# A feed-forward that starts its output blocks by chunks, one weight tile per reciprocal, and constant matmuls around a layer norm's broadcast

## The reference

```python
def _conv_ffn(h, w_up, conv_w, conv_b, w_down):
    gate, val = jnp.split(h @ w_up, 2, axis=-1)          # D_FF = 2816
    gate = lax.conv_general_dilated(gate, conv_w[:, None, :], (1,), ...) + conv_b
    return (jax.nn.silu(gate) * val) @ w_down

# a layer, for x and (in layer 0) for the context
x = _layer_norm_2(DEEPNORM_ALPHA * x + g1 * y, ln1_g, ln1_b)
h = x * (1.0 + sc2) + sh2
x = _layer_norm_2(DEEPNORM_ALPHA * x + g2 * _conv_ffn(h, ...), ln2_g, ln2_b)
# layer 0 before its attention: q and k get an RMS norm per head of 64, then a rotation
qa = _rope(_rms_norm_2(_heads(qa, 8, 64), q_gain), cos, sin)
```

## Time and profile before

| | us |
|---|---|
| median of 3 runs | 1800.74 (1795.88 to 1807.39) |
| the profiled execution: its time | 1801.82 |
| its span | 1800.0 |
| PE busy | 1646.7, 91% |
| DVE busy | 940.6, 52% |
| ACT busy | 745.1, 41% |
| granted TensorE clock, mean | 0.962 |

### The profile page before, as it was taken

The page is one execution under the profiler, slowest core; times in us unless marked ns, Lnnn a source line. Parts: engine busy times, 40 slices in busy tenths (PEclk is TensorE's granted clock), DMA queues, the critical chain, the costliest instruction groups (busy, mean ns, idle before and its releaser), DMA issues.

```text
span 1800.0 us, 37019 instructions
## 1 busy us (share of the span) xinstructions
PE 1646.7 (91%) x14957; PEld 1326.6 (74%) x14957; DVE 940.6 (52%) x1712; ACT 745.1 (41%) x1411; POOL 170.8 (9%) x270
## 2 busy tenths in 40 slices
PE   6888899896898988999999899999998999989997
PEld 6675678695666665867666788788875877879997
DVE  5743663486623223264665655335534564578584
ACT  6231444453211124423764533323334556565454
POOL 0020010004000000100431100000001002210000
PEclk9999999997999999999999899999998999989998
DMA  6598777769599998212002222222222240235552
GB/s 248 182 243 280 263 256 250 271 196 265 224 406 407 401 361 296 89 59 83 2 13 82 70 94 94 94 94 94 94 82 71 94 141 13 72 120 181 183 174 71
DMA packets 84418, 302.04 MB, mean 168 GB/s; under 512 B 10080, under 2 KB 12128, under 8 KB 84128
## 3 DMA queue, kind: packets, MB, share of 16 engines
q1 hardware_dynamic: 80144, 288.92, 45.9%
q0 software_dynamic: 2736, 7.35, 1.7%
q10 hardware_dynamic: 1376, 3.47, 0.5%
HBM read 345.56 MB, written 3.15 MB: 194 GB/s over the span
## 4 chain that ended last, share of the span: by engine, by line
PE 77%; DVE 10%; DMA 4%; ACT 4%; issue 3%; POOL 0%; ACTq 0%; SPq 0%; DVEq 0%
PE bank L941 51%; PE bank L900 13%; PE bank L1435 5%; DMA ring<-wall 4%; PE bank L1470 3%; PE bank L1455 3%; PE bank L965 2%; DVE w_lo L2194 2%; ACT w_hi L1684 1%; DVE BIG L2820 1%; PE bank L1447 1%; PE bank L1491 1%; ACT BIG L1754 0%; DVE SV L2244 0%; DVE BIG L2415 0%
## 5 line engine op out<-in xcount | busy, mean ns | idle before, releaser
L941 PE MATMUL bank<-BIG_f32r,w_hi 128*128 128x256 f32 (+1 forms) x2208 | 551.2, 339 | 21.0 <-DVE BIG_f32r L2209 15.6
L2194 DVE TENSOR_TENSOR w_lo<-ring,w_hi 128x1024 fp32r<-128x1024 f32 x261 | 323.9, 1250 | 329.7 <-ACT w_hi L1684 328.4
L941 PEld LDWEIGHTS bank<-BIG_f32r,w_hi 128*128 128x128 f32 x2208 | 381.0, 191 | 71.7 <-issue 23.2
L941 PE MATMUL bank<-BIG_f32r,w_lo 128*128 128x256 f32 (+1 forms) x1136 | 385.9, 340 | 0.0
L1684 ACT ACTIVATE w_hi<-ring 128x1024 fp32r<-128x1024 f32 x261 | 272.7, 1054 | 230.3 <-PE bank L941 159.2
L941 PE MATMUL bank<-AR_f32r,w_hi 128*128 128x256 f32 (+1 forms) x1050 | 273.4, 336 | 9.1 <-DVE AR_f32r L2209 7.4
L941 PEld LDWEIGHTS bank<-BIG_f32r,w_lo 128*128 128x128 f32 x1136 | 217.3, 191 | 25.6 <-issue 0.5
L941 PEld LDWEIGHTS bank<-AR_f32r,w_hi 128*128 128x128 f32 x1050 | 183.7, 191 | 34.3 <-DVE AR_f32r L2209 8.7
L941 PE MATMUL bank<-AR_f32r,w_lo 128*128 128x256 f32 (+1 forms) x440 | 147.5, 335 | 0.0
L941 PE MATMUL bank<-XC_f32r,w_lo 128*128 128x256 f32 x424 | 122.2, 288 | 0.0
L941 PE MATMUL bank<-XC_f32r,w_hi 128*128 128x256 f32 x424 | 122.0, 288 | 0.0
(11 more groups left out here) (368 smaller groups left out, 2254.2 us busy)
## 6 DMA issues: line engine op xcount, KB each, us to landing
ring<-wall SPq DMA_DIRECT2D x451, 512.0 KB, 4.4
BIG<-wall SPq DMA_DIRECT2D x92, 512.0 KB, 9.5
w_extra<-wall ACTq DMA_DIRECT2D x15, 2048.0 KB
w_extra<-wall ACTq DMA_DIRECT2D x15, 1024.0 KB
BIG<-t_rows POOLq DMA_DIRECT2D x16, 128.0 KB, 11.1
AR<-na_rows POOLq DMA_DIRECT2D x32, 64.0 KB, 7.2
w_extra<-wall SPq DMA_DIRECT2D x1, 2048.0 KB
na_rows<-rpb_pad POOLq DMA_DIRECT2D x1, 1792.0 KB, 30.0
```

The source lines that it names most:

```text
L941: ins = nc.tensor.matmul(o, l, r, start=start and n == 0, stop=stop and n == 2, **kw)
L2194: V.tensor_tensor(w_lo[:, i % SPLIT_RING, :], ring[:, t % RING, :], w_hi[:, i % SPLIT_RING, :].bitcast(F32), ALU.subtract).then_inc(w_spli ...
```

## The change

Three edits in layer 0's input projection, four feed-forward halves and four norms.

1. PE no longer waits for all 11 chunks ahead of the output blocks. The first block (m = 0) waits for chunk k before its three matmuls of chunk k; the other seven wait for nothing more.
2. In the input projection DVE's loop over the reciprocals calls `feed("l0in", 8 + m)`, so that a tile is split before each of the reciprocals 1 to 4, and two tiles are split within the rotation's loop. PE makes block 13 ahead of the rotations; the list `plan` follows.
3. PE gets matmuls whose result nobody reads (`idle_products`: 256 columns, plain float32, two constants): 2 between the last of the `var` sums and the wait for the reciprocal in norms b to e (8 in all), and 4 (b, e) or 6 (c, d) ahead of the pair that follows (20 in all). The true products then overwrite the bank.

```diff
         L0_ORDER = [("l0in", m) for m in range(7)] + [("qms", m) for m in range(5)] \
-            + [("l0in", m) for m in range(7, 13)] + [("rope0", m) for m in range(5)] \
-            + [("l0in", 13)] + [("l0vals", t) for t in range(4)]
+            + [("l0in", m) for m in range(7, 14)] + [("rope0", m) for m in range(5)] \
+            + [("l0vals", t) for t in range(4)]
...
+            def idle_products(o, count):
+
+                for _ in range(count):
+                    mm(o[:, 0:S], c_("ones"), c_("causal")[:, 0:S])
...
                 b = open_(("rs", which))
+                if which in LN_NEXT:
+                    idle_products(b, 2)
                 pe.wait_ge(sem("ln_recip"), nth(which) + 1)
...
             def split_pair(names, stage, n0, x, os, ready):
 
+                idle_products(os[0], 6 if stage in ("l0upA", "l1in") else 4)
...
-                    pe.wait_ge(sem("ff_split"), l * FF + (half + 1) * HF)
                     for m in range(KC):
                         b = open_((f"l{l}down", half, m))
-                        split_linear((f"l{l}down", half, m), f"l{l}down{part}", m * HF, HF, u, b[:, 0:n])
+                        split_linear((f"l{l}down", half, m), f"l{l}down{part}", m * HF, HF, u, b[:, 0:n],
+                                     None if m else (sem("ff_split"), l * FF + half * HF))
...
             for m in range(5):
-                feed("l0in", 8 + m // 2)
+                feed("l0in", 8 + m)
                 dve.wait_ge(sem("q0_rms"), m + 1)
                 step(V.reciprocal(tq[:, m, :], tq[:, m, :]))
...
                 step(V.tensor_tensor(Q0[:, m, 0:S], Q0[:, m, 0:S], tq[:, m, 0:S], ALU.add), "q0_roped")
+                if m in (1, 3):
+                    feed("l0in", 14 + m // 2)
             feed("l0in", 17)
```

## The result

The changed kernel took 1780.17 us (median of 4 runs, 1775.79 to 1782.36) against 1799.74 us for the kernel before (4 runs, 1795.88 to 1807.39): a ratio of 0.9883, 95% interval 0.9845 to 0.9921. The forecast was 1779 us. Two later measurements of the same kernel gave 0.9866 (0.9841 to 0.9892) and 0.9903 (0.9872 to 0.9934); the mean of the three savings is 1.16%, 21 us.

The account below looks back on a forecast made before the run. PE bounds the kernel, busy 91% of the span, so only its pauses and half clock pay. 10.7 + 5.4 + 6.3 = 22.4 us off 1801.82 gives 1779.4, adjusted to 1779; own range 1773 to 1783, whole range 1772 to 1790.

Parts of the forecast that it names:

- Part 1: Feed-forward output halves: chunk waits remove PE's four pauses and the half clock behind two; 10.7 us, bounds 8 to 12.
- What I said would be late next: Last feed-forward half, layer 1: PE waits for the second weight tile, giving back about 1.0 us.
- the 1.7 us that I took for the clock: Second half of layer 0's feed-forward: half clock behind the 2.44 us gap goes, 63.43 - 61.7 = 1.7 us.
- Part 2: Input projection: one tile split per reciprocal removes PE's pause (3.6 us) and half clock (1.8); 5.4 us, bounds 3 to 5.5.
- Rival C: Input projection: the pause moves, as splits take 1.6 instead of 1.2 us; gain 2 instead of 5.4, time 1782; chance 0.08.
- Part 3: Norms b to e: unread matmuls fill PE's pauses and avoid half clock afterwards; 6.3 us, bounds -5 to 8.5.
- rival A: Norms: the unread matmuls bring nothing; 16.1 us gained in all, time 1784.6; chance 0.20.
- rival B: Norms: the unread matmuls stay at half clock and are late by 5.1 us; time 1790; chance 0.06.
- my ceiling of 3.0: Norm b: at most half of the 5.9 us stretch at clock 0.50 after the norm can be won, 3.0 us.
- The 8.5 us for part 3: Norms: by the skill's rule filled gaps count as activity, so all four norms give their ceiling, 8.5 us.
- my own case: Whole kernel: the forecast of 1779 us with its own range 1773 to 1783; chance 0.58.
- Faster by over 1%: Whole kernel: time below 1782.7 us; chance 0.60, against 0.37 for within 1% and 0.03 for slower.

Follow-up runs that it names:

- e1_part1: Only the chunk waits of the first output blocks added to the kernel before: 1788.74 us, ratio 0.9903.
- e2_part2: Only the new order of weight tiles and of block 13 in the input projection, added to the kernel before: 1798.66 us, ratio 0.9976.
- e3_part3: Only the unread matmuls added to the kernel before: 1796.28 us, ratio 0.9960.
- e8_waits: The changed kernel with chunk waits in all eight output blocks of each half, 308 more waits: 1781.46 us in a single run.
- a_after: The changed kernel measured again, unedited: 1779.21 us, ratio 0.9866 to the kernel before.
- a_after2: The changed kernel measured once more, unedited, on another run's chip: 1784.6 us, ratio 0.9903 to the kernel before.
- e4_parts12: The changed kernel without the unread matmuls: 1784.31 us, ratio 0.9885 to the kernel before.

## Why the prediction was right, point by point

**Part 1, the output blocks: 10.7 forecast, 10.39 measured.** All four pauses of the earlier trace rows are gone. What I said would be late next is late: the second weight tile of the last half. In the changed kernel, PE (first fence) and DVE (second):

```profile
1730.43 0.36 PE L941 MATMUL bank<-AR_f32r,w_hi 128*128 128x256 f32 x1 [0.86 <-DVE w_lo L2202]
```

```profile
1729.06 2.36 DVE L2202 TENSOR_TENSOR w_lo<-ring,w_hi 128x1024 fp32r<-128x1024 f32 x2 [0.59 <-ACT w_hi L1692]
```

DVE's pair of splits is the one of the earlier trace rows, at the same distance from its last rests, and PE stands still for 0.86 us where I had 1.0. `e1_part1` repeats all four stages to 0.01 us. One half of this sum is less firm than I wrote. The gap of 2.44 us in layer 0 is followed by a half clock in the kernel before but not in every execution that has the gap. The same place in `e2_part2`, where the pause is 2.44 us as well, and in the kernel before:

```profile
1297.90:1301.30 3.40, 3.40 (x15) 1.00 0.22 45
```

```profile
1312.04:1315.40 3.36, 3.36 (x10) 0.50 0.43 150
```

That is 15 matmuls of the same kind against 10. The stage took 16.01 us in the one and 17.56 in the other (17.32 in `e3_part3`, again with half clock), so the edit wins 2.7 or 4.25 us there, by the execution: the 1.7 us that I took for the clock come in some executions only.

**Part 2, the input projection: 5.4 forecast, 5.38 measured**, 65.93 to 65.95 us in every kernel that has the edit. The order of DVE's work runs as worked out, in the changed kernel:

```profile
801.52 1.23 DVE L2202 TENSOR_TENSOR w_lo<-ring,w_hi 128x1024 fp32r<-128x1024 f32 x1
802.66 3.35 DVE L2828 RECIPROCAL BIG<-BIG 128x512 f32<-128x512 f32 x1
806.04 0.75 DVE L2830 SCALAR_TENSOR_TENSOR AR<-AR,par,BIG 128x512 f32<-128x512 f32 x1
```

The fifth round ends at 806.79, and the rotations start at 808.22: 1.4 us to spare where I had 1.2. Rival C had this margin used up; each split took 1.23 us, not the 1.6 that C needs. The rule "one split per reciprocal" works because a round with a split, 5.31 us, is shorter than the 5.6 us that PE takes for a tile.

**Part 3, the unread matmuls: 6.3 forecast, 7.4 in the first profile, 5.3 over all executions.** This is the least well sized term. The four norm stages add up to 96.76, 97.08, 98.07, 97.10 and 99.37 us in the five executions with the matmuls (changed kernel, `e3_part3`, `e8_waits`, `a_after`, `a_after2`; mean 97.68), and to 104.12, 102.36, 102.87 and 102.40 in the four without (before, `e1_part1`, `e2_part2`, `e4_parts12`; mean 102.94). The two groups don't overlap, and in all 20 norms of the five executions the pair starts at full clock, in all 16 of the four at half clock. So rival A (nothing) and rival B (late) fall, but the gain differs by 2 to 3 us from one execution to the next, because the clock is still low in some of the norms. By place the first profile has b 1.97 (2.6 forecast), c 2.18 (2.3), d 2.73 (1.7), e 0.48 (0.2); the means of the two groups give b 1.6, c 1.8, d 2.0 and e -0.1. So b and c were sized too high, d a little too low, and in e the unread matmuls bring nothing, although the pair there starts at full clock too: its broadcast comes 1.43 to 1.94 us behind the last sum where it came 1.11 us behind it in the kernel before, which is lateness of the sort that rival B priced. I had put d lowest for its size because there the clock was at 0.50 through the sums. That still holds in the changed kernel, and yet the clock is up when the pair starts (the window from 1372.20 above). Within the norm, ahead of the pair:

```profile
1359.80:1366.50 6.70, 6.24 (x68) 0.50 0.10 18
```

That the matmuls "bring it up during the pair at best" was the step that was too careful for d: they bring it up before. For b it goes the other way by the execution: 23.32 us in `a_after` and `e8_waits`, 3.06 less than before and my ceiling of 3.0, but 24.41 to 24.56 in the other three, where its sums met the half clock.

The Trainium skill, page "TensorE: Matmul & The Clock Gate", section "What's actually happening" of Part 1, has activity release the throttle. The windows at 1.00 behind all four norms agree with it. The 8.5 us for part 3 that I had by it did not come: it was 7.4 in the first profile and 5.3 on average, since some sums and broadcasts ahead of the pairs still run at 0.50, as the window above shows for d, with PE busy for 6.24 of 6.70 us.

**The sum.** 10.4 + 5.4 + 5.3 = 21.1 us by the stages, 20.9 by the mean of the three ratios, 22.4 forecast. The mechanisms of all three parts are the ones that the prediction named. That the first median, 1780.17, lies 1.2 us from the forecast is in part luck: the same kernel later had medians of 1779.21 and 1784.6 us, and the last is outside the 1773 to 1783 that I gave my own case. "Faster by over 1%" held in this measurement and in the second, and the third shows 0.97%: the 0.60 against 0.37 was about how open that was. Places that I could not see did meet the clock at another moment, as I had allowed for with 1 us: the attention of layer 1 and the feed-forward behind norm e, 141.79 and 59.22 us in place of 143.25 and 57.70. In the first profile they happen to cancel.

## What to carry to other kernels

Where a consumer waits for all its inputs at once, look at how long its own first part takes: if it uses them in the order in which they come, one wait per input costs nothing measurable (308 met waits, under 0.1 us), and the tail of the producer is hidden; then ask what is late next, here a weight tile. A pause of TensorE can cost twice, once for itself and once for the half clock after it; matmuls that nobody reads can fill it, but they have to stand ahead of the wait and be shorter than the pause, also where the clock is low and they take twice as long: doubling them took back all that they had won, and in norm e even the single number won nothing. Judge edits of this size by stages between fixed events: whole times of one kernel scattered by 12 us over six runs and by 23 over ten, while the stages of edits 1 and 2 repeated to 0.02 us. Where an edit's gain hangs on the clock, as in the norms, one execution is not enough even so: the four norms took 96.76 to 99.37 us.

## What the runs showed of the hardware that I had not expected

- The same pause does not have the same effect in every execution. After 2.44 us in layer 0 the clock was at 0.50 in the kernel before and in `e3_part3`, and stayed at 1.00 in `e2_part2`. The attention of layer 1, with the same code, took 141.7, 143.2, 144.7 or 149.4 us, and 0, 3.4, 6.8 or 17.1 us of it ran at half clock. What decides it, I did not settle.
- In the changed kernel a piece at half clock stands in layer 1's feed-forward where PE is busy without a gap:

```profile
1578.22:1581.63 3.41, 3.41 (x19) 0.50 0.79 284
```

  It begins 1.4 us after a pause of 1.76 us for a weight tile had ended, not at the pause. In `a_after` the same pause left the clock at full, and the stage took 57.70 instead of 59.22 us. So what happens in a slow piece need not be its cause; the pause shortly before it is a candidate, but `a_after` shows that it does not always have this effect.
- The part from the start to norm b, identical in all kernels, took from 703.31 to 725.70 us. That is as much as the whole change brings, and probably a reason why its interval is as wide as it is. I did not look into it further; the stages behind it are free of it.
